# Multiplying constants on TensorE while it waits, in a two-layer hybrid decoder step

## The reference

```
layer 0: h += mixer0(rms_norm(h));  h += swiglu(rms_norm(h))
  q, k, v = x @ w_in0                      # 16 heads of 64
  heads 0-7:  stick-breaking attention     # sigmoids, cumulative products
  heads 8-15: MoBA                         # blocks of 256 keys chosen by gate, softmax
  out = concat(heads) @ w_out0
layer 1: h += mixer1(rms_norm(h));  h += swiglu(rms_norm(h))
  q (16 heads), k/v of three branches (4 heads each), gates = x @ w_in1
  compressed branch: blocks of 32 keys through a two-layer MLP (cmp_w1, cmp_w2)
  selected branch:   16 blocks of 64 keys, chosen by the compressed scores
  window branch:     the last 512 keys
  out = (gated sum of the three) @ w_out1
outputs: y and the new keys and values, for the prompt and the samples
```

## Time and profile before

| | us |
|---|---|
| median of three timed executions | 1347.74 (1347.23 to 1352.3) |
| profiled execution, its own time | 1351.01 |
| its span, first to last instruction | 1349.3 |
| TensorE busy in the span | 1263.9 (94%) |
| VectorE / ScalarE / GpSimd busy | 766.8 (57%) / 331.8 (25%) / 251.6 (19%) |
| mean granted clock of TensorE | 0.973 |
| share of TensorE in the chain that ended last | 83% |

### The profile page before, as it was taken

The page is one execution under the profiler, slowest core; times in us unless marked ns, Lnnn a source line. Parts: engine busy times, 40 slices in busy tenths (PEclk is TensorE's granted clock), DMA queues, the critical chain, the costliest instruction groups (busy, mean ns, idle before and its releaser), DMA issues.

```text
span 1349.3 us, 26130 instructions
## 1 busy us (share of the span) xinstructions
PE 1263.9 (94%) x10044; PEld 1013.5 (75%) x10044; DVE 766.8 (57%) x1644; ACT 331.8 (25%) x819; POOL 251.6 (19%) x327
## 2 busy tenths in 40 slices
PE   7997898968899999999999999998889899999998
PEld 4454576746788888799999975565545578999998
DVE  1803745675567672377777428656434318768754
ACT  2123634433243321110000002256633311000000
POOL 0103000044332430212111011034023121112100
PEclk9999799989899999999999999998899999999999
DMA  7337788796654755335444532552056654544351
GB/s 261 135 115 256 254 326 296 273 290 211 203 181 165 247 193 178 125 125 163 151 131 140 198 125 69 187 162 80 18 171 223 215 187 142 170 130 164 129 172 36
DMA packets 151070, 236.11 MB, mean 175 GB/s; under 512 B 10626, under 2 KB 113282, under 8 KB 150530
## 3 DMA queue, kind: packets, MB, share of 16 engines
q1 hardware_dynamic: 138914, 203.09, 45.0%
q0 software_dynamic: 7872, 29.26, 6.4%
q10 hardware_dynamic: 4160, 2.10, 0.5%
HBM read 229.09 MB, written 13.64 MB: 180 GB/s over the span
## 4 chain that ended last, share of the span: by engine, by line
PE 83%; DVE 7%; ACT 3%; issue 2%; DMA 2%; SPq 2%; POOL 0%; POOLq 0%; DVEq 0%; ACTq 0%
PE ps L817 20%; PE ps L600 12%; PE ps L845 11%; PE ps L565 11%; PE ps L912 8%; PE ps L783 5%; PE ps L795 2%; PE ps L707 2%; PE ps L1074 2%; PE ps L606 2%; PE ps L759 2%; ACT big L1205 1%; PE ps L1115 1%; DMA ring<-in_cache_kv 1%; SPq L437 1%
## 5 line engine op out<-in xcount | busy, mean ns | idle before, releaser
L565 PE MATMUL ps<-ct,ring 128*128 128x128 f32 x960 | 142.0, 285 | 22.2 <-DMA ring<-in_cache_kv 9.4
L600 PE MATMUL ps<-ring,xT 128*128 128x512 f32 (+1 forms) x384 | 161.7, 577 | 0.9 <-DMA ring<-in_w_in 0.9
L565 PEld LDWEIGHTS ps<-ct,ring 128*128 128x128 f32 x960 | 109.0, 144 | 65.0 <-issue 42.3
L912 PE MATMUL ps<-big,proj 128*128 128x168 f32 (+1 forms) x896 | 138.1, 307 | 1.8 <-DVE big L1917 1.8
L912 PEld LDWEIGHTS ps<-big,proj 128*128 128x128 f32 x896 | 129.3, 190 | 4.9 <-issue 4.4
L600 PEld LDWEIGHTS ps<-ring,xT 128*128 128x128 f32 x384 | 70.5, 193 | 80.3 <-issue 78.3
L817 PE MATMUL ps<-kT,proj 128*128 128x144 f32 x960 | 124.1, 286 | 0.0
L817 PEld LDWEIGHTS ps<-kT,proj 128*128 128x128 f32 x960 | 120.3, 190 | 0.0
L1205 ACT ACTIVATE big<-ps 128x512 f32<-128x512 f32 (+2 forms) x158 | 84.5, 553 | 101.7 <-PE ps L565 100.5
L2221 POOL TENSOR_TENSOR big<-rows 128x576 f32<-128x576 f32 x22 | 51.0, 2319 | 261.4 <-DVE rows L1813 228.1
L817 PE MATMUL ps<-xT,ring 128*128 128x144 f32 x640 | 84.9, 286 | 0.0
(11 more groups left out here) (310 smaller groups left out, 2104.1 us busy)
## 6 DMA issues: line engine op xcount, KB each, us to landing
ring<-in_cache_kv SPq DMA_DIRECT2D x128, 512.0 KB, 5.7
ring<-in_w_gu SPq DMA_DIRECT2D x44, 1024.0 KB, 7.6
ring<-in_w_in SPq DMA_DIRECT2D x11, 2048.0 KB, 7.9
ring<-in_w_down SPq DMA_DIRECT2D x16, 1408.0 KB, 6.5
ring<-in_cache_kv SPq DMA_DIRECT2D x128, 128.0 KB, 3.4
ring<-in_cache_kv POOLq DMA_DIRECT2D x128, 128.0 KB, 3.3
ring<-in_w_out SPq DMA_DIRECT2D x4, 2048.0 KB, 10.6
ring<-in_state_win SPq DMA_DIRECT2D x16, 512.0 KB, 5.4
```

The costliest lines, as they stand in the source:

```text
L565: return nc.tensor.transpose(out, in_, C("ident", 0, rows, rows))
L600: last = mm(ps[b + t][:, 0:w], xT[:, k, t * P:(t + 1) * P], src[:, k, :], start=k == 0, stop=k == KD - 1)
L912: last = mm(cmp_out(u, si, n), w, XS[(4 * kp + si) % XB][:, o, 0:n], start=o == 0, stop=o == 7)
```

## The change

A helper `fill(bank, n, w)` multiplies the identity with the first w columns of the constants, n times, into a PSUM bank whose content nobody needs at that point. Nothing reads what it writes. It is called in layer 0's prompt stage before every turn of weights (w = 256), before the first turn of the first page set (7 times 512 columns), before value steps (1, 1) and (1, 2) (2 each), in layer 1's prompt stage before pair 0's turns (2), before pair 2's scores (1) and before pair 1's turns (2), and in layer 1's decode before group 1's new scores (2), before group 3's turned weights (1) and before the last turned output (1). Some calls have waits before them, so that the bank is free and the constants have landed. No other engine's program is changed, and no DMA.

```diff
--- before.py
+++ after.py
@@ -564,6 +564,11 @@
             def turn(out, in_, rows=P):
                 return nc.tensor.transpose(out, in_, C("ident", 0, rows, rows))
 
+            def fill(bank, n, w=512):
+
+                for _ in range(n):
+                    mm(bank[:, 0:w], C("ident"), ct[:, 0:w], start=True, stop=True)
+
             pe.wait_ge(s_io, 64)
             for j in range(2):
                 for t in range(3):
@@ -675,7 +680,11 @@
                             scores(j + 1)
                         values(j - 1)
                     if j < NH // 2:
+                        if j >= 2:
+                            pe.wait_ge(a_oe[0], j - 1)
+                        fill(ps[4 + j % 2], 1, 256)
                         turn_w(2 * j)
+                        fill(ps[4 + j % 2], 1, 256)
                         turn_w(2 * j + 1)
 
             def decode_k0():
@@ -1027,12 +1036,16 @@
 
                 prompt_scores(1)
                 for j in range(NH // 2 + 1):
+                    if j == 1:
+                        fill(ps[6], 1)
                     if 1 <= j and j + 1 < NH // 2:
                         prompt_scores(j + 1)
                     if j >= 2:
                         values(j - 1)
                     if j == 2:
                         turn_compressed(1)
+                    if j < 2:
+                        fill(ps[6], 2)
                     if j < NH // 2:
                         turn_w(2 * j)
                         turn_w(2 * j + 1)
@@ -1125,6 +1138,7 @@
             pe.wait_ge(in_e[0], 3 * len(nin[0]))
             pe.wait_ge(in_q[0], full_chunks(0, 5))
             pe.wait_ge(t_e[0], 12)
+            pe.wait_ge(s_const, 80)
             prompt0()
             decode_k0()
             for step in steps:
@@ -1136,10 +1150,17 @@
                     if step[1] == 5:
                         pe.wait_ge(r_te[0], 12)
                 elif step[0] == "v":
+                    if step[1:] in ((1, 1), (1, 2)):
+                        fill(ps[7], 2)
                     values0(*step[1:])
                 elif step[0] == "back":
                     turn_o(0, step[1])
                 elif step[0] == "turned":
+                    if step == ("turned", 0, 0):
+                        pe.wait_ge(s_const, 80)
+                        pe.wait_ge(k_a[0], 64)
+                        pe.wait_ge(k_d[0], 64)
+                        fill(ps[6], 7)
                     turn_cmp(*step[1:])
                 elif step[0] == "second":
                     second(step[1])
@@ -1176,17 +1197,23 @@
                         turn_k1(src, 2 * g + 2, i)
                 if g >= 1:
                     values1(g - 1)
+                if g == 0:
+                    fill(ps[5], 2)
                 if g < 3:
                     compressed_and_new(g + 1)
                     src = take(pe, "k1", 2 * g + 3)
                     for i in range(6):
                         turn_k1(src, 2 * g + 3, i)
+                if g == 3:
+                    pe.wait_ge(r_ps[1], 4)
+                    fill(ps[0], 1)
                 turn_weights1(g)
                 if g < 3:
                     importance(g + 1)
                 if g >= 1:
                     turn_o(1, g - 1)
             values1(3)
+            fill(ps[0], 1)
             turn_o(1, 3)
             pe.wait_ge(v_e[1], 4)
             project_out(1)
```

## The result

The changed kernel takes 1341.66 us (median of 18 runs, 1338.35 to 1351.21); the kernel before took 1349.44 us (18 runs, 1343.38 to 1353.96). The ratio is 0.9956, 95% interval 0.994 to 0.9971: 3.9 to 8.1 us less, 5.9 us in the middle; the two medians lie 7.8 us apart. The forecast was 8.4 us less at 1339.3 us; rival A was priced at 5 us less.

What follows compares the result with a forecast made beforehand. TensorE was taken as busy almost throughout, with 31 us the ceiling from 71.8 us of half clock. Terms summed to 9.4 us, taken as 8.4 us against the median: 1339.3 us, range 1333.5 to 1346 (8 in 10).

Steps and rivals of the forecast that it cites:

- rival A: Where fills leave rest gaps, the clock may fall anyway; 5 us less against the median, 1342.8 us; chance 0.20.
- The signs named beforehand: If right: full clock about 130-163, 286-292, 330-333, 345-350, 992, 1067-1084 us; value step two 1.9 us; page set DMA-ended.
- Layer 0's prompt: Layer 0's prompt stage: 1.1 us at scores, 1.75 us at stage end, less 0.85 us of delays; 2.0 us saved.
- First page set: Eight turns after the page wait: three rounds at full clock give 1.4 us; two thirds taken for remaining rest, 0.9 us.
- Value step (1,1): First value step: falls from 3.60 to 1.92 us, but the next instruction's DMA wait grows to 2.3 us; worth 0.
- Value step (1,2): Second value step: full clock on the work behind gives 2.6 us; 1.7 us taken as 2.8 us of rest remain.
- Layer 1's first heads: Layer 1's prompt: fills make the turn 1.0 us late, full clock behind gives 3.1 us; 1.0 us taken.
- rival C: Fills delay ScalarE's copies behind turns in layer 0 and layer 1's first pairs, VectorE waits; 7 us slower, 1355; chance 0.05.
- Decode: Layer 1's decode: 1.2 us at group 1's new scores, 1.1 us at group 3's weights, 1.5 us at output projection.
- rival B: Gain swallowed because VectorE or a DMA is late next everywhere; 2 us or less, 1346; chance 0.09.
- Waits: Three new waits before fills, for constants, kept keys and read scores, are already satisfied; all costed at 0.
- D: Multiplying by the identity does not hold the clock up; gains 0, costs 1 to 2 us, 1349; chance 0.06.

Runs made afterwards that it cites:

- l1_only: The changed kernel with only layer 1's fills (prompt heads 0 to 3, three places in decode); 1346.62 us, ratio 0.9982 to the kernel before.
- p0_512: The changed kernel with the 16 fills of layer 0's prompt stage at 512 columns instead of 256; 1343.44 us, ratio 0.9958 to the kernel before.
- steps_only: The changed kernel with only the fills of the first page set and the two value steps; 1347.02 us, ratio 0.9976 to the kernel before.
- placed: The changed kernel with early's matmuls, fewer layer 0 prompt fills, layer 1's first fills behind first turns, and further fills elsewhere; 1336.22 us, ratio 0.9905.
- P1_moved: The changed kernel with fills of layer 1's pairs 0 and 1 behind each pair's first turn (two, three) instead of before it; 1341.51 us, one execution.
- by_turns: The changed kernel with fills made of transposes of the identity, seven per 512 columns, instead of matmuls; 1342.47 us, ratio 0.9946 to the kernel before.
- v12_only: The changed kernel with value-step fills only before step (1, 2), not before (1, 1); 1337.29 us, one execution.
- early: The changed kernel plus three 512-column matmuls of a tile of ones while TensorE waits for the first inputs; 1344.88 us, ratio 0.9954 to the kernel before.

## Why the prediction came out as it did

The direction and the mechanism are shown: the clock stayed up behind most fills, and where work without a wait follows, half of its time came back. The measured 5.9 us lie between rival A (5) and the forecast (8.4, just outside the interval); they are under the 6.7 us (0.5%) that I had set for telling a change from none, though the interval stays clear of none. The signs named beforehand came out mixed: full clock at 130 to 163, at 345 to 350, at 992 and at 1067 to 1084 as said, but half clock at 285.6 to 289.0 and again at 917.1. A's rest gaps held in some places and not in others. Step by step:

- *Layer 0's prompt, forecast 2.0 us.* The term that came out wrong. The stage itself took 0.18 us more. The scores at 145.44 were worth 0.4 us of VectorE's waiting, not 1.1 us: it waited 0.41 us for them before, and not at all now. The end of the stage gave 1.03 us (3.68 to 2.65 us), not 1.75. Against that stands VectorE's one wait for ScalarE, 1.14 us before and 2.55 us now; 0.95 us of the 1.41 us are the fills', near the 0.85 us taken off, and the rest goes with the first half clock, which lasted 6.8 us for 3.4 us. Over the kernels the stage took 42.73 or 42.74 us without these fills (42.94 us before) and 42.10 to 43.15 us with all of them. Behind the stage the keys gave 1.06 us, since the clock no longer falls at 156 to 163. Net 0.9 us in this profile; the timed runs without and with them (0.9978 and 0.9956) stand 3 us apart, with room for 0 to some 6 us, and l1_only had no such fall without any fill. The Trainium skill (same page, Part 1) says that the point at which the clock moves is not tied to the kernel's start; these profiles agree: the clock first rose at 19.6 us in the kernel before and at 12.5 us in the changed one, with the same work up to there, and the unchanged start differs by 2.59 us.
- *First page set, forecast 0.9 us, 1.4 with the clock up.* 7.87 to 7.43 us, 0.44, with the clock down at 285.6 in spite of the fill; p0_512, steps_only and placed, with no fall there, took 6.73 to 6.74 us: 1.14. P1_moved and by_turns, with 6.8 us of half clock there, gained nothing (7.84 and 7.88 us). The bounds and the two cases of A were right.
- *Value step (1,1), forecast 0.* The gain went into the wait for the DMA as said. But in most kernels with both fills the next load came earlier, and 0.8 to 1.1 us were saved up to (1, 2) in five of the kernels with both.
- *Value step (1,2), forecast 1.7 us.* Measured 2.55 us (27.97 to 25.42 us) in nine of the ten kernels with a fill here; placed took 27.05 us, with a fall at 339.7 all the same. I had discounted the full 2.6 us for 2.8 us of rest between fill and step. In the changed kernel there was no rest, since the load came earlier, and where there was (2.44 us in v12_only, 2.95 us in by_turns), the clock held. Mis-sized.
- *Layer 1's first heads, forecast 1.0 us.* 1.59 us measured (34.27 to 32.68 us), 1.5 to 3.2 us over the six kernels with the fills in this place and full clock on the compressed scores. The delay of 1.0 us in the forecast's sum did not show: VectorE's sum stands 9.94 us behind the start of the compressed scores, 10.31 us before. But rival C is real here: where half clock came as the compressed scores ended, the fills made pair 2's scores 1.2 us later (l1_only), and early and by_turns, with 6.8 us of it, took 3.3 and 2.8 us more for the stretch than before the change.
- *Decode, forecast 1.2, 1.1 and 1.5 us.* Measured 0.0, 0.96 and 1.69 us (the last in ten of the eleven kernels with that fill, not in placed). At group 1 the softmax on VectorE and ScalarE is late next; its wait took the whole gain (0.70 to 2.23 us). That is rival B, at one place, and I had not asked there what is late next.
- *Waits, forecast 0.* No wait of more than 0.3 us stands ahead of a fill in the changed kernel's waits.
- *D* is out: behind fills of constants (25.42 us for 27.97) and of transposes (the same) the clock held, and behind early's ones it first rose at 7.4 us.

With the chance parts left out (2.59 us and 1.82 us), the profile's terms are -0.18 + 1.06 + 0.44 + 1.08 + 2.55 + 1.59 + 0.0 + 0.96 + 1.69 = 9.2 us, near the forecast's 9.4 us, by errors that cancel. With the chance parts they come to the profile's 9.97 us. The timed difference is 5.9 us by the ratio and 7.8 us by the medians: the profiled execution of the kernel before was 1.6 us slower than its median, that of the changed kernel 0.6 us faster. The rest is what one profiled execution does not tell: falls of the clock that come elsewhere in another execution, and that a fill may only move. Pair 2 to 7 and group 0 to 2 show it. Where the first had no fall (28.86 us for 31.5), the second had one in four of five kernels (52.72 to 54.45 us for 50.52), and only placed, with fills in both, had neither. That this makes up the gap is argued, not shown.

## What to carry to other kernels

Fill a wait of TensorE with constants only where the work behind it is TensorE's own path for at least as long as the half clock would last, and where the wait is longer than the fill at half clock; behind it, ask of every place what is late next. Put the fill behind the instruction that another engine waits for, not before it: with the clock up the place made next to no difference (0.17 us); with the same half clock as the compressed scores ended it made 1.8 us at the first turn (9.58 against 7.79) and 1.2 us at the next scores (14.65 against 13.50). Look for the fill in the chain too: in layer 0's prompt stage VectorE's wait for ScalarE grew by 0.95 us. Judge by timed rounds and by a table of stretches over several kernels, since one unchanged stretch, the start, differs by up to 3.8 us from profile to profile.

## What the hardware showed that was not expected

- Half clock often comes after the wait, on the work behind it. In the changed kernel it began at 302.7, 0.5 us behind the end of a wait of 1.92 us (below), and at 333.4, 0.8 us behind the end of one of 2.35 us; in early at 14.2, 1.2 us behind one of 2.78 us. TensorE was busy 3.40 of 3.40 us in the first two.

```profile
302.17 0.65 PE L565 MATMUL ps<-ct,ring 128*128 128x128 f32 x4 [1.92 <-DVE kT L1926]
```

- A fall can also come with no wait ahead, during narrow matmuls. The compressed scores (32 matmuls of 30 columns) had one at their end or shortly before it in five of the thirteen kernels: before (903.7), l1_only (901.5), early (898.2), by_turns (899.7) and placed (896.0).
- A fall seems to be moved as easily as removed: without one before pair 7, most kernels had one in group 0 to 2.
- The records show no level ahead of their first change. In the kernel before the first eight projection instructions took 6.77 us from 13.40 on, 0.85 us each, twice the 0.43 us of the earlier trace rows, while the granted clock is given as 1.00 (second fence, behind the busy times of the five engines). The clock's first recorded rise is at 19.6 us there and at 12.5 us in the changed kernel, with nothing changed ahead of it.

```profile
13.40 6.77 PE L600 MATMUL ps<-ring,xT 128*128 128x512 f32 x8 [0.87 <-DMA ring<-in_w_in]
```

```profile
12.00:19.00 7.00, 6.13 (x11) 2.90 (x12) 4.15 (x11) 4.90 (x11) 2.40 (x1) 1.00 1.06 373
```
